# Moving the last eight modulation tiles of a fused hybrid-mixer block from GpSimd and ScalarE, inside the recurrence, to VectorE behind it

## The reference: one layer of a conditioned mixer and a gated feed-forward

```python
mod = cond @ w_ada[l] + b_ada[l]                  # cond = silu(c)
sh1, sc1, gt1, sh2, sc2, gt2 = split(mod, 6)
h = rms_norm(x, g_pre_mix[l]) * (1.0 + sc1) + sh1
cv_val, cv_gate, q, f, i, og = split(h @ w_in[l]) # 1024 x 3072
out_a = conformer_conv(...)                       # gated, 31 taps, layer norm, swish
out_b = hgrn2(q, f, i, og, ...)                   # 4 heads, gated linear recurrence
mix = concatenate([out_a, out_b]) @ w_out[l]
x = x + gt1 * rms_norm(mix, g_post_mix[l])
h2 = rms_norm(x, g_pre_ffn[l]) * (1.0 + sc2) + sh2
gate, up = split(h2 @ w_ffn_in[l]); y = (silu(gate) * up) @ w_ffn_out[l]
x = x + gt2 * rms_norm(y, g_post_ffn[l])
```

## Time and profile before

| | |
|---|---|
| median of 3 runs | 1121.51 us (1120.98 to 1121.74) |
| the profiled execution: its time, and the span of its trace | 1123.33 us, 1120.8 us |
| TensorE busy, share of the span | 1079.6 us, 96% |
| VectorE, GpSimd, ScalarE busy | 826.1, 779.6, 501.9 us |
| transfers | 108.00 MB, mean 96 GB/s |

### The profile page before, as it was taken

One profiled execution on the slowest core, in us unless ns is written; L12 is line 12 of the kernel. 1 busy time (PEld: TensorE's weight loads), 2 busy tenths in 40 slices (PEclk: granted clock), 3 DMA queues, 4 the chain that ended last, 5 costly groups with the idle time before them and its releaser, 6 DMA issues.

```text
span 1120.8 us, 14373 instructions
## 1 busy us (share of the span) xinstructions
PE 1079.6 (96%) x5043; PEld 893.3 (80%) x5043; DVE 826.1 (74%) x1155; ACT 501.9 (45%) x853; POOL 779.6 (70%) x673
## 2 busy tenths in 40 slices
PE   2899999999999999999999999999999999999996
PEld 1678888888877888888888888888888888888885
DVE  5987997979998745678775767676666666666658
ACT  5755565574652834345333333233333333333334
POOL 7658967667773630427977777778686869696966
PEclk9999999999999999999999999999999999999998
DMA  9624324232321271212222222222221212212217
GB/s 344 223 79 146 104 85 125 83 115 72 96 75 39 76 250 69 94 39 85 83 71 62 70 63 75 67 70 72 60 74 59 79 60 70 72 60 73 67 51 295
DMA packets 98744, 108.00 MB, mean 96 GB/s; under 512 B 6541, under 2 KB 76402, under 8 KB 98674
## 3 DMA queue, kind: packets, MB, share of 16 engines
q1 hardware_dynamic: 97216, 102.79, 28.8%
q10 hardware_dynamic: 1458, 4.31, 1.0%
HBM read 98.68 MB, written 8.40 MB: 96 GB/s over the span
## 4 chain that ended last, share of the span: by engine, by line
PE 83%; DVE 6%; ACT 2%; issue 2%; POOL 1%; DMA 1%; DVEq 0%; ACTq 0%
PE pair L2180 34%; PE pair L2200 17%; PE pair L1989 16%; PE pair L2089 8%; PE pair L2143 2%; PE pair L2223 2%; PE pair L2022 1%; DVE qk L1544 1%; DVE tt L1537 1%; DMA ada<-in_w_ada 1%; DVE pair L1507 1%; DVE qk L1551 1%; POOL ada L746 1%; DVE pmat L1560 1%; PE pair L2017 1%
## 5 line engine op out<-in xcount | busy, mean ns | idle before, releaser
L1808 DVE TENSOR_TENSOR yt<-yt,pair 128x512 f32<-128x512 f32 x264 | 176.1, 683 | 35.3 <-PE pair L2200 35.3
L746 POOL TENSOR_TENSOR ada<-ada,cond 128x256 f32<-128x256 f32 x128 | 101.8, 828 | 64.2 <-DMA ada<-in_w_ada 64.0
L844 POOL TENSOR_TENSOR raw_r<-raw,w_hi 128x512 fp32r<-128x512 f32 x68 | 96.2, 1415 | 65.0 <-ACT w_hi L1263 65.0
L1507 DVE SCALAR_TENSOR_TENSOR pair<-u,conv_w_col,pair 128x512 f32<-128x512 f32 x208 | 139.6, 746 | 1.9 <-ACT pair L1127 1.4
L2200 PE MATMUL pair<-w_lo,op_hi 128*128 128x512 f32 x280 | 109.1, 389 | 0.0
L2200 PE MATMUL pair<-w_hi,op_lo 128*128 128x512 f32 x280 | 109.0, 389 | 0.0
L2200 PE MATMUL pair<-w_hi,op_hi 128*128 128x512 f32 x280 | 108.9, 389 | 0.0
L853 POOL TENSOR_TENSOR w_lo<-w_lo_f,w_hi 128x512 fp32r<-128x512 f32 x70 | 95.3, 1362 | 0.0
L2180 PE MATMUL pair<-t_lo,w_hi 128*128 128x512 f32 x240 | 93.7, 390 | 0.0
L2180 PE MATMUL pair<-t_hi,w_hi 128*128 128x512 f32 x240 | 93.4, 389 | 0.0
L1263 ACT ACTIVATE w_hi<-raw 128x512 fp32r<-128x512 f32 x68 | 42.6, 626 | 73.0 <-PE pair L2180 71.8
(11 more groups left out here) (327 smaller groups left out, 3007.8 us busy)
## 6 DMA issues: line engine op xcount, KB each, us to landing
ada<-in_w_ada SPq DMA_DIRECT2D x48, 512.0 KB, 4.8
raw<-in_w_ffn_in SPq DMA_DIRECT2D x56, 256.0 KB, 2.9
raw<-in_w_in SPq DMA_DIRECT2D x24, 512.0 KB, 5.5
w_lo_f<-in_w_ffn_out SPq DMA_DIRECT2D x40, 256.0 KB, 3.0
w_hi_f<-in_w_ffn_out SPq DMA_DIRECT2D x30, 256.0 KB, 3.1
x<-in_x SPq DMA_DIRECT2D x8, 512.0 KB, 8.0
raw<-in_w_out SPq DMA_DIRECT2D x8, 512.0 KB, 3.4
x<-in_x SPq DMA_DIRECT2D x4, 1024.0 KB, 8.8
```

What stands on the lines that cost most here:

```text
L746: i_ = pool.tensor_tensor(ada[:, n % ADA_RING, cols], ada[:, n % ADA_RING, cols], cond[:, cols], ALU.mult)
L844: pool.tensor_tensor(place_part(at), place_full(at), place_part(GU_HIGH[m % 3]), ALU.subtract).then_inc(gu_low, 1)
L1507: i_ = dve.scalar_tensor_tensor(out=dst, in0=tap_of(j + 1, h), scalar=tap_weight(j + 1, t), in1=dst, op0=ALU.mult, op1=ALU.add)
L1808: i_ = dve.tensor_tensor(dst, dst, bank(4 + t), ALU.add)
```

## The change

Tiles 24 to 31 of the 32, those of `gt2`, leave the recurrence. The ring now serves 24 tiles, six in each period instead of eight (two, one, two and one with four chunks, where there were two with each). The eight others have four buffers of their own, `ada_late`, in the place of the late taps' and keys' buffers, which are free by then. VectorE does product and sum of each in one instruction (`late_tile`, L1739 of the changed kernel), behind `mix_low` and ahead of `residual(0)`, and then adds the bias and makes the second gain (`late_gain`). `cond` moves to another address. On SP the loads of the first four late tiles stand ahead of the `w_out` chunks, those of the other four behind the loads of `x1` and ahead of the feed-forward's weights, and each of these four waits until the tile that had its buffer is summed. The second gain is stored near the end of the program instead of with the first.

```diff
+ADA_ROWS = 3 * KT
+ADA_LATE = 4
 def ada_rows(g):
     t, c = divmod(g - 1, 5) if g > 5 else (0, g - 2)
-    return [KT * t + 2 * c, KT * t + 2 * c + 1] if t < 4 and 0 <= c < 4 else []
+    if t >= 4 or not 0 <= c < 4:
+        return []
+    first = ADA_ROWS // 4 * t + (0, 2, 3, 5)[c]
+    return list(range(first, first + (2, 1, 2, 1)[c]))
...
+        _, ada_late, cond = group([("before_ada_late", [P, 2 * (N_OUT - WS) + TT + 6, D], F32),
+                                   ("ada_late", [P, ADA_LATE, D], F32), ("cond", [P, D], F32)])
...
-            sp.wait_ge(mod_ready, 3)
-            for call in range(2):
+            def store_gain(call):
+
+                sp.wait_ge(mod_ready, call + 2)
                 sp.dma_start(gg_d[call:call + 1, :].rearrange("o (kt p) -> (o p) kt", p=P), gg[:, call, :],
                              allow_slow_non_contiguous=True
                              ).then_inc(gg_stored, 16)
-            sp.wait_ge(gg_stored, 32)
+                sp.wait_ge(gg_stored, 16 * (call + 1))
+
+            def load_late(n):
+
+                if n >= ADA_LATE:
+                    sp.wait_ge(late_summed, n - ADA_LATE + 1)
+                sp.dma_start(ada_late[:, n % ADA_LATE, :], w_ada_d[:, 5 * KT + n, :]).then_inc(late_loaded[n % ADA_LATE], 16)
+            store_gain(0)
             load_gain(0, ggb[:, :])
+            sp.wait_ge(*slot_done(3, KDT_LAST))
+            sp.wait_ge(*bank_freed(3, KDT_LAST - 2))
+            sp.wait_ge(tap_done, HEADS * TAP_STEPS)
+            for n in range(ADA_LATE):
+                load_late(n)
             for g in range(N_IN + WS, N_IN + N_OUT):
                 load_chunk(g)
...
                 sp.dma_start(x1[:, 2 * i:2 * i + 2, :], x_d[:, 2 * i:2 * i + 2, :]).then_inc(x1_loaded[i], 16)
 
 
+            for n in range(ADA_LATE, KT):
+                load_late(n)
             for n, (kind, f) in enumerate(PLAIN):
...
             sp.wait_ge(x1_stored, 16 * TT)
+            store_gain(1)
             apart(sp, (gu_done, N_STEPS))
             load_gain(1, w_hi_f[:, 0, :])
...
+            def late_tile(n):
+
+                dve.wait_ge(late_loaded[n % ADA_LATE], 16 * (n // ADA_LATE + 1))
+                src = ada_late[:, n % ADA_LATE, :]
+                dve.scalar_tensor_tensor(out=src, in0=src, scalar=1.0, in1=cond[:, :], op0=ALU.mult, op1=ALU.mult,
+                                         accum_out=mod[:, 5 * KT + n:5 * KT + n + 1]).then_inc(late_summed, 1)
+
+            def late_gain():
+
+                dve.wait_ge(late_summed, KT)
+                me.done(dve.tensor_tensor(mod[:, 5 * KT:6 * KT], mod[:, 5 * KT:6 * KT],
+                                          vec[:, ROW_BADA + 5 * KT:ROW_BADA + 6 * KT], ALU.add))
+                me.wait()
+                dve.tensor_tensor(gg[:, 1, :], mod[:, 5 * KT:6 * KT], vec[:, ROW_GPOST2:ROW_GPOST2 + KT], ALU.mult
+                                  ).then_inc(mod_ready, 1)
+            for n in range(KT):
+                late_tile(n)
+            late_gain()
             for i in range(TT):
                 residual(i)
```

More of the change, by code:

```diff
@@ L245, in build @@
         x0, ada0 = group([("x0", [P, TT, D], F32), ("ada0", [P, ADA_FIRST, 2, D], F32)])
-        qk, f, tt, vt, v, pmat, kdt, state, on, ot, y4, og, ada, cond, sg, u, masks_late, keys, late_taps, late_next = group([
+        qk, f, tt, vt, v, pmat, kdt, state, on, ot, y4, og, ada, sg, u, masks_late, keys, late_taps, late_next = group([
             ("qk", [P, 2, S], F32), ("f", [P, S], F32), ("tt", [P, S], F32), ("vt", [P, S], F32),
@@ L249, in build @@
             ("on", [P, TT, P], F32), ("ot", [P, HEADS, S], F32), ("y4", [P, CT, S], F32), ("og", [P, S], F32),
-            ("ada", [P, 2, D], F32), ("cond", [P, D], F32), ("sg", [P, S], F32), ("u", [P, S + TAPS - 1], F32),
+            ("ada", [P, 2, D], F32), ("sg", [P, S], F32), ("u", [P, S + TAPS - 1], F32),
             ("masks_late", [P, len(HALVES), P // 2], F32), ("keys", [P, 2, HALF], F32), ("late_taps", [P, S], F32), ("late_next", [P, 2, S], F32)])
         ln_sum_, ln_sum_sq, ln_sq = sg, u[:, 0:S], ada
+        _, ada_late, cond = group([("before_ada_late", [P, 2 * (N_OUT - WS) + TT + 6, D], F32),
+                                   ("ada_late", [P, ADA_LATE, D], F32), ("cond", [P, D], F32)])
         wo_hi, wo_lo, x1, xs, tail_tmp = group([
@@ L321, in build @@
         ada_summed = sem("ada_summed")
+        late_loaded = [sem(f"late_loaded{i}") for i in range(ADA_LATE)]
+        late_summed = sem("late_summed")
         ring_free = sem("ring_free")
@@ L551, in load_ada @@
             def load_ada(n):
-                if n >= 32:
+                if n >= ADA_ROWS:
                     return
@@ L1147, in ln_step @@
                     if t == 0:
-                        act.wait_ge(ada_summed, 4 * KT)
+                        act.wait_ge(ada_summed, ADA_ROWS)
                     if t >= 2:
@@ L1181, in _ @@
                         ln_step(piece)
-                    if k in (4, 6) and ada_rows(g - 1):
-                        ada_sum(ada_rows(g - 1)[k // 2 - 2])
+                    if k in (4, 6):
+                        for n in ada_rows(g - 1)[k // 2 - 2:k // 2 - 1]:
+                            ada_sum(n)
             def swish(t):
@@ L1658, in _ @@
                     if period == 4 and piece == 18:
-                        dve.wait_ge(ada_summed, 4 * KT)
-                        me.done(dve.tensor_tensor(mod[:, 2 * KT:6 * KT], mod[:, 2 * KT:6 * KT],
-                                                  vec[:, ROW_BADA + 2 * KT:ROW_BADA + 6 * KT], ALU.add))
+                        dve.wait_ge(ada_summed, ADA_ROWS)
+                        me.done(dve.tensor_tensor(mod[:, 2 * KT:5 * KT], mod[:, 2 * KT:5 * KT],
+                                                  vec[:, ROW_BADA + 2 * KT:ROW_BADA + 5 * KT], ALU.add))
                         me.wait()
@@ L1666, in _ @@
                         dve.tensor_tensor(gg[:, 0, :], mod[:, 16:24], vec[:, ROW_GPOST1:ROW_GPOST1 + KT], ALU.mult
-                                          ).then_inc(mod_ready, 1)
-                        dve.tensor_tensor(gg[:, 1, :], mod[:, 40:48], vec[:, ROW_GPOST2:ROW_GPOST2 + KT], ALU.mult
                                           ).then_inc(mod_ready, 1)
```

## The result

The changed kernel takes **1130.96 us** (median, 1129.38 to 1132.67), the kernel before 1122.15 us beside it: ratio 1.0072, interval 1.0056 to 1.0087, so 8.8 us slower. The forecast was 1130.9 us, from a median before of 1121.5: 9.4 us more. The profiled execution took 1131.77 us, its span is 1129.9 us.

What follows compares the result with a forecast made beforehand. TensorE's pace bounds the kernel, with 4.33 us idle in the recurrence and 0.36 us slack ahead of tile 4. Stall 9.4 plus clock 1.4 less gain 1.4 gave +9.4 us: 1130.9 from 1121.5, range 1127.0 to 1135.0.

Steps and rivals of the forecast that it cites:

- A: Forecast at 80%: the second four late loads queue behind `x1` on SP's queue; 1130.9 us, for single terms off 1128 to 1134.5.
- The first four tiles: VectorE behind its low parts: sums of 1.3 us, two perhaps 3 us beside GpSimd, ending between 404.0 and 407.5.
- The second four, the term that decides: SP's queue: late tiles 4 to 7 land one behind the other after `x1`, tile 7 at 417.3, at most 419.4.
- One sum: VectorE's late product and sum: one instruction of 1226 ns and a read of 77 ns, 1.3 us; half throughput not taken.
- The stall: `residual(0)` starts at 419.0 instead of 409.27, 9.7 us late; TensorE loses 9.4 us ahead of output tile 4.
- The second gain's store: Near the program's end: done by 1086.0 at worst, load behind it at 1089.11; hidden by 3.1 us, cost 0.
- rival D: Worse, 7%: the second gain's store isn't hidden and delays the last gain; 1134 us with 3 us excess, 1137 with 6.
- Two costs that were set to nothing: Ahead of `residual(0)`: nothing waits for the first four late loads, and GpSimd's low parts, perhaps 3.28 us, cost nothing.
- A sign of being wrong that came true: SP's late loads: the prediction called itself wrong if late tile 4 landed before 410.
- The recurrence's gain: Less GpSimd work beside VectorE, priced in the last head: 1.4 us gained, bounds 0 and 4.3.
- The clock: TensorE's clock falls in the gap ahead of output tile 4: 1.4 us lost, bounds 0.7 and 2.8.
- Rival C: Faster, 5%: VectorE's idle stretch ahead of `residual(0)` holds all eight sums; 1117.2 us, needing tile 7 landed before about 408.

Runs made afterwards that it cites:

- the late sums in the gaps: Changed kernel with four late sums kept ahead of `residual(0)` and the other four moved behind residuals 1 to 3: 1118.70 us, ratio 0.9964 to the kernel before.
- the relief alone: Changed kernel without the eight late tiles' loads and sums, the second gate being its bias alone: 1118.76 us, ratio 0.9962 to the kernel before.
- the late part alone: Changed kernel with all 32 tiles back in the ring, the last eight done again late: 1133.32 us, ratio 1.0089 to the kernel before.
- the loads behind the first of `x1`: Changed kernel with the second four late loads behind `x1`'s first load instead of its fourth: 1125.89 us, ratio 1.0032 to the kernel before.
- all loads ahead: Changed kernel with eight late buffers and all eight late loads ahead of the `w_out` chunks: 1122.77 us, ratio 1.0001 to the kernel before.
- the kernel with `cond` moved: Kernel before, 32 tiles in the ring and no late part, only `cond` at its address in the changed kernel: 1122.37 us, ratio 1.0011.
- a full ring and the gaps: Changed kernel with four late sums moved behind residuals 1 to 3 and all 32 tiles in the ring: 1122.39 us, ratio 0.9999 to the kernel before.

## Why the prediction was right

**The forecast's mechanism, A, held.** The second four tiles stood behind `x1`, VectorE waited until 414.40, and TensorE had one gap ahead of tile 4.

- *The first four tiles:* sums of 3.42, 3.40, 1.21 and 1.22 us, and the end at 404.2. Predicted: two of about 3 us, the end between 404.0 and 407.5. The number fits only by chance: VectorE's low parts ended 3.6 us earlier, and from their end on the four took 9.0 us, a little over the 8.7 of the late bound.
- *The second four, the term that decides:* tile 7 was there by 414.40. The prediction's 417.3 moves to 413.7 with the 3.6 us that everything came earlier: right within 0.7 us. Moving these loads took away 8.2 us of 8.8, so this was tested and not only read. The Trainium skill's rule against which it was weighed (DMA: Bandwidth & Descriptors, Specifications), a limit of about 358 GB/s, doesn't show here either: 410 GB/s in 402 to 410.
- *One sum:* 1.23 us for 1024 columns. That this form runs at half throughput with two float32 inputs in SBUF (the Trainium skill, Vector Engine (DVE) Microarchitecture Reference, Points that are easy to get wrong) shows in no trace here: it took 1.21 to 1.23 us in the six places where GpSimd was idle, and 3.4 us in the two beside GpSimd.
- *The stall:* `residual(0)` at 415.96 (419.0 less 3.6 is 415.4), TensorE's gap 9.71 us (9.4).
- *The second gain's store:* its load went out at 1098.15, 16.0 us behind the store and 9.0 us later than at 1089.11, no more than the program as a whole had moved. The store itself landed within 10.3 us. It was hidden; rival D didn't happen.
- *Nothing made up behind it:* 630.00 of 630 us busy.
- *A sign of being wrong that came true:* late tile 4 landed at 409.7, and the prediction named a landing before 410. The mark was set in the times of the old trace; with everything 3.6 us earlier it would have been 406.4, and the wait came as forecast.

**Two terms were too small, and they cancel.** The recurrence's gain was taken as 1.4 us and is 3.3 (timed alone); the bounds of 0 and 4.3 held it. The step that failed is the one from a single instruction in the last head to the whole recurrence: the heads ahead of it gave another 1.0 to 2.0 us. What the prediction looked for as its sign, about 1 us of idle time in 320 to 340, was 1.69, since the work in that fixed window had moved; heads would have been the better ruler. The clock was taken as 1.4 us, from the start of the kernel, and is 1.7 to 2.6; the bounds of 0.7 and 2.8 held it. That it falls was read rightly, but the 2.8 us at the start rest on the lengths of matmuls alone: the granted clock in the windows there is 1.00. So the median came out within 0.1 us by luck: with the right gain alone it would have been 1129.0. A part of the luck is the base, three runs with a median of 1121.5 where fifteen gave 1122.15; forecast was +9.4 us, measured +8.8.

**Two costs that were set to nothing.** The prediction put the first four loads and GpSimd's stretched low parts at 0. That was right, and not only under cover of the 9.7 us: with the late sums in the gaps both stand as in the changed kernel, TensorE waits for neither, and the time (1118.70) is that of the relief alone (1118.76). It doesn't hold for eight loads in that place: there they cost TensorE 2.0 us, and the eight sums 1.0 us. Rival C (the hole holds it all, 1117.2) was therefore further off than a landing in time: no kernel here with eight sums ahead of `residual(0)` got under 1122.

**Left open:** 0.5 us of the time with the loads behind the first of `x1`, 1.0 us of the one with all loads ahead, and the 0.8 us by which gap and clock exceed the timed cost of the late part alone. Of the full rings the time together spreads from 205.6 to 207.7 us between single traces, which is of that size, but this doesn't show that it is the cause.

## What to carry to other kernels

A hole in an engine's timeline isn't free room if the chain behind it has little slack (0.36 us here): look instead for the short pauses that recur in an exchange between engines, where one sum of 1.2 us a tile cost nothing. A load that is written at the right moment of the program still lands behind everything that its queue already holds, so add up the bytes ahead of it, 4 MB here, before counting on it. And price contention over all instructions that run beside the work taken away, head by head, not from one pair of rows, and up to the bottleneck's own pace only. When an engine stops without a releaser, look at the lengths of the other engines' instructions just ahead of it.

## What was not expected of the hardware

- **The clock falls in a short gap and comes back at different lengths.** It fell in a single gap of 4.50 us, and did not fall in the kernel with 3.0 us of waits in three pieces. Behind gaps of 9.7 and 9.85 us it stayed at the lower level for 5.3 and 4.4 us, behind the 4.5 us one for 2.7. What decides this length the runs don't show.
- **VectorE with two inputs from SBUF and GpSimd take turns.** Alone a 128x1024 takes VectorE 1.21 us and GpSimd 2.40. In the changed kernel VectorE's low part stands at 394.02 and its first two sums at 395.16 and 398.51 (3.42 and 3.40 us). GpSimd's low parts beside them:

```profile
394.31 3.19 POOL L939 TENSOR_TENSOR wo_lo<-raw,wo_hi 128x1024 fp32r<-128x1024 f32 x1 [1.29 <-ACT wo_hi L1233]
397.71 3.13 POOL L939 TENSOR_TENSOR wo_lo<-raw,wo_hi 128x1024 fp32r<-128x1024 f32 x1 [0.21 <-ACT wo_hi L1233]
```

  They end at 397.50 and 400.84, each 2.3 us behind the end of VectorE's instruction that ran when they began; VectorE's sums end at 398.58 and 401.91, each 1.1 us behind GpSimd's. So in these rows neither is slowed by a factor: each waits for the other to end and then takes about its own time.
- **In a few executions the turn doesn't come for 11 us.** Two profiled executions, of the kernel with `cond` moved (1134.04 us) and of the one with a full ring and the gaps (1133.61 us), show TensorE idle for 8.5 and 8.3 us ahead of the same matmul of the first head, put down to "issue". The cause stands on VectorE. In the first of them:

```profile
107.51 12.45 DVE L1587 TENSOR_TENSOR qk<-qk,f 128x1024 f32<-128x1024 f32 x1 [0.16 <-PE pair L2018]
```

```profile
108.14 2.83 POOL L737 TENSOR_TENSOR w_lo<-raw,w_hi 128x256 fp32r<-128x256 f32 x4
110.93 5.51 POOL L747 TENSOR_TENSOR ada<-ada,cond 128x256 f32<-128x256 f32 x8
116.39 2.49 POOL L764 TENSOR_TENSOR late_taps<-late_taps,late_next 128x512 f32<-128x512 f32 x2
```

```profile
120.06 2.05 PE L2023 MATMUL pair<-qk,keys 128*128 128x128 f32 x8 [8.50 <-issue]
```

  This instruction makes the queries and counts up the semaphore `level` that the matmul waits for. It took 12.45 us where the same one took 2.17 in the kernel before. It ended at 119.96, 1.1 us behind the last of fourteen instructions that GpSimd ran from 108.14 on without a pause, and faster than in the kernel before (the first four in 2.83 us instead of 5.36). TensorE starts 0.1 us behind it, at the lower clock (granted 0.79 in 120 to 130). The other execution has the same rows, with 12.30 us. These two were 11 to 12 us longer than their kernels' medians, and the table above uses only differences between places behind the stop. Four executions of kernels with a full ring that were not traced are as long (1132.4 to 1134.0 us), and none of the 82 with a lighter ring is. What lets GpSimd keep its turn in these executions the runs don't show.
